# Expert weights and rows brought in at the ends of earlier stages, and a hidden transpose moved from TensorE to VectorE

## The reference, cut to what matters

```python
def ec_ffn(h, router_w, w_gate, w_up, w_down):
    cap = EC_CAPACITY_FACTOR * n_tok // N_EXPERTS
    aff = jax.nn.softmax((h @ router_w).astype(jnp.float32), axis=-1)
    top_aff, idx = lax.top_k(jnp.swapaxes(aff, 1, 2), cap)
    xg = jax.vmap(lambda hb, ib: hb[ib])(h, idx)
    hid = jax.nn.silu(xg @ w_gate) * (xg @ w_up)            # per expert, 1024 -> 512
    y = (hid @ w_down) * top_aff[..., None]                 # 512 -> 1024
    return zeros.at[idx].add(y)
```

```python
def hier_moe(h, w_rg, b_rg, w_re, b_re, w_up, w_down):
    grp = argmax(h @ w_rg + b_rg); p_grp = softmax(...)[grp]
    top_v, top_i = lax.top_k((h @ w_re + b_re)[grp], TOP_K)        # TOP_K = 2
    gate = jax.nn.softmax(top_v, axis=-1) * p_grp
    g, u = jnp.split(xb @ w_up[e], 2, axis=-1)                     # 1024 -> 2 x 512
    y = (jax.nn.silu(g) * u) @ w_down[e]                           # 512 -> 1024
    return segment_sum(y * gate, token)
```

## Time and profile before

| what | us |
|---|---|
| median of three runs (4654.29 to 4656.44) | 4656.21 |
| the profiled execution | 4653.48 |
| its span in the trace | 4651.7 |
| PE busy in the span | 4087.7 (88%) |
| DVE busy | 2057.1 (44%) |
| ACT busy | 1237.6 (27%) |
| POOL busy | 732.8 (16%) |
| data moved by DMA | 761.18 MB, mean 164 GB/s |

### The profile page before, as it was taken

The page is one execution under the profiler, slowest core; times in us unless marked ns, Lnnn a source line. Parts: engine busy times, 40 slices in busy tenths (PEclk is TensorE's granted clock), DMA queues, the critical chain, the costliest instruction groups (busy, mean ns, idle before and its releaser), DMA issues. The chain is left out here.

```text
span 4651.7 us, 76558 instructions
## 1 busy us (share of the span) xinstructions
PE 4087.7 (88%) x30623; PEld 2783.0 (60%) x30623; DVE 2057.1 (44%) x4137; ACT 1237.6 (27%) x2473; POOL 732.8 (16%) x851
## 2 busy tenths in 40 slices
PE   6998999976999799899986997999887987799995
PEld 4674557444887567566544885767565645455553
DVE  1223557126555322456425453121396676444443
ACT  1112346140000111335330001111265433233333
POOL 0110000301111011000201110000362050122221
PEclk8998999987999899999988998999898998899997
DMA  7115110357787511412138996210352102899996
GB/s 256 35 47 130 24 34 16 131 207 290 269 278 276 164 54 45 110 24 49 40 148 329 335 331 231 88 56 31 104 137 90 42 32 85 311 378 361 367 374 237
DMA packets 247019, 761.18 MB, mean 164 GB/s; under 512 B 60836, under 2 KB 137196, under 8 KB 233256
## 3 DMA queue, kind: packets, MB, share of 16 engines
q1 hardware_dynamic: 219240, 653.77, 39.2%
q0 software_dynamic: 21808, 81.80, 7.0%
q10 hardware_dynamic: 5712, 22.02, 1.2%
HBM read 646.28 MB, written 111.25 MB: 163 GB/s over the span
## 5 line engine op out<-in xcount | busy, mean ns | idle before, releaser
L627 PE MATMUL p_ring<-p_hT,p_wc 128*128 128x256 f32 x1008 | 220.3, 381 | 4.9 <-DMA p_wc<-in_w_in 4.9
L3507 ACT ACTIVATE bexp_y<-bexp_acc,slot_gates 32x256 f32<-32x256 f32 x384 | 178.8, 466 | 144.3 <-PE bexp_acc L3550 135.5
L3565 PE MATMUL bexp_gu<-bexp_wu,bexp_xT 128*32 128x256 f32 x3072 | 182.1, 395 | 39.1 <-DMA bexp_wu<-in_w_expert_up 34.6
L627 PEld LDWEIGHTS p_ring<-p_hT,p_wc 128*128 128x128 f32 x1008 | 192.2, 191 | 31.6 <-issue 5.3
L3565 PE MATMUL bexp_gu<-X,bexp_xT 128*32 128x256 f32 x3072 | 177.8, 389 | 14.5 <-DMA X<-in_w_expert_up 11.7
L3594 DVE TENSOR_SCALAR bexp_ex<-bexp_ex 128x128 f32<-128x128 f32 x96 | 53.3, 555 | 287.4 <-ACT bexp_ex L3515 287.3
L635 PE MATMUL p_ring<-p_wt,p_hT 128*128 128x400 f32 (+2 forms) x480 | 170.8, 516 | 0.0
L3565 PEld LDWEIGHTS bexp_gu<-bexp_wu,bexp_xT 128*32 128x32 f32 x3072 | 101.4, 114 | 114.3 <-issue 58.5
L1119 PE MATMUL l0mla_scores<-l0mla_kT,l0mla_qT 96*128 96x512 f32 (+1 forms) x312 | 143.0, 547 | 21.0 <-DMA l0mla_qT<-RT 15.2
L2029 PE MATMUL l0exp_gu<-l0exp_xT,l0exp_wg 128*128 128x160 f32 x1024 | 154.4, 304 | 4.5 <-DVE l0exp_xT L2073 4.5
L3565 PEld LDWEIGHTS bexp_gu<-X,bexp_xT 128*32 128x32 f32 x3072 | 98.9, 112 | 87.8 <-DMA X<-in_w_expert_up 17.1
(11 more groups left out here) (683 smaller groups left out, 8436.6 us busy)
## 6 DMA issues: line engine op xcount, KB each, us to landing
X<-in_w_expert_up SPq DMA_DIRECT2D x16, 4096.0 KB, 18.5
bexp_wu<-in_w_expert_up SPq DMA_DIRECT2D x16, 4096.0 KB, 18.5
l0exp_wg<-in_exp_w_gate SPq DMA_DIRECT2D x16, 2048.0 KB, 8.4
l0exp_wu<-in_exp_w_up SPq DMA_DIRECT2D x16, 2048.0 KB, 13.1
l0exp_wd<-in_exp_w_down SPq DMA_DIRECT2D x16, 2048.0 KB, 12.9
l1exp_wg<-in_exp_w_gate SPq DMA_DIRECT2D x16, 2048.0 KB, 8.8
l1exp_wu<-in_exp_w_up SPq DMA_DIRECT2D x16, 2048.0 KB, 13.1
l1exp_wd<-in_exp_w_down SPq DMA_DIRECT2D x16, 2048.0 KB, 13.9
```

What stands on the lines that cost most here:

```text
L627: mm = nc.tensor.matmul(out[:, i * PC:(i + 1) * PC], wc[:, k, b * 128:(b + 1) * 128], hT[ch % 2][:, k, :], start=(k == 0), stop=(k == KD - 1))
L3507: nc.scalar.activation(y[j][32 * r:32 * r + 32, c * YN:(c + 1) * YN], acc[rows_c, r // 2, r % 2, :], ACT.Copy, scale=gates[rows_c, r, bass ...
L3565: mm = nc.tensor.matmul(gu[r][32 * c:32 * c + 32, 0:2 * HN].rearrange("p (h n) -> p h n", h=2), xT[j][:, k, 32 * r:32 * r + 32], both[:, : ...
```

## The change

**First experts.** A class `FirstExpert` owns three 4 MB buffers `held` and a buffer of rows across both the route and the experts stage. The modulation weights of the route pass through `held`, each half of which is later one expert weight buffer; the rows' buffer is also the route's `hT0`. At the end of the route SP issues the weights of expert 0 once the modulation products that used those buffers are done, and POOL issues expert 0's gathers once the rows are stored and the choice is written. In the experts stage SP waits until they have landed and goes on with expert 1, and POOL gathers for expert 1.

```diff
+    def load(self, sp, multiplied, groups):
+        sp.wait_ge(multiplied, START + groups - 2)
+        sp.dma_start(self.wg[0], ...).then_inc(self.gate_in, 16)
+        sp.dma_start(self.wu[0], ...).then_inc(self.up_in, 16)
+        sp.wait_ge(multiplied, START + groups - 1)
+        sp.dma_start(self.wd[0], ...).then_inc(self.down_in, 16)
...
-                for n in range(N):
+                for n in range(N - 1):
                     mod.store(sp, n)
+                expert.load(sp, mod.multiplied, N)
+                mod.store(sp, N - 1)
                 mod.wait_end(sp)
-                for j in range(3):
-                    sp.wait_ge(stored[j], START + 16 * len(range(j, NT, 3)))
...
                 for n in range(N):
                     mod.finish(po, n)
+                for j in range(NX):
+                    po.wait_ge(stored[j], START + 16 * len(range(j, NT, NX)))
+                po.wait_ge(final_taken, START + 2 * len(sets))
+                expert.gather(po, XN)
...
-                for e in range(E):
+                sp.wait_ge(gathered[0], 16 * NS)
+                for e in range(1, E):
...
-                for e in range(B):
-                    gather(e)
+                gather(1)
```

```diff
+                act.dma_start(first_up[0], w_up[0]...).then_inc(first_in[0][0], 16)
+                for e in range(2):
+                    act.dma_start(first_down[e], w_down[e]...).then_inc(first_in[1][e], 16)
                 act.wait_ge(eps_made, START + 1)
...
-                step(V_.tensor_scalar(nb[:, :], cnt[:, 0:N_EXP], 0.0, None, ALU.is_gt))
-                for q in range(1, -(-SEQ // BLOCK)):
-                    step(V_.scalar_tensor_tensor(nb[:, :], cnt[:, 0:N_EXP], float(BLOCK * q), nb[:, :], ALU.is_gt, ALU.add))
+                step(V_.tensor_tensor(counted_over[:, :, :], over..., cnt..., ALU.is_lt))
+                step(V_.tensor_reduce(more[:, :], counted_over[:, :, :], AX.X, ALU.add))
...
+                    po.wait_ge(steps, START + marks[f"blocks{half}"])
+                    nc.gpsimd.tensor_tensor(pair[:, part, 1, :], in_block[:, part, :], gate..., ALU.mult).then_inc(spread, 1)
...
-                sp.wait_ge(steps, START + marks["first"])
+                sp.wait_ge(squares, START + T)
                 sp.wait_ge(spilled, START + 16 * T)
-                sp.dma_start(first_w[0], w_up[e]...); sp.dma_start(first_w[1], w_down[e]...)
+                sp.dma_start(first_up[1], w_up[1]...).then_inc(first_in[0][1], 16)
```

```diff
-                with sp.Fori(1, pairs) as i:
-                    for j in range(B):
-                        ...
+                load_up(1, 0)
+                with sp.Fori(1, last) as i:
+                    load_up(i, 1)
+                    load_down(i, 0)
+                    load_up(i + 1, 0)
+                    load_down(i, 1)
+                load_up(last, 1)
+                load_down(last, 0)
+                load_down(last, 1)
...
-                        if r == 0 and not first:
-                            hid_turn(i + j - 1, 1 - j)
...
+                        nc.vector.tensor_tensor(hidR[j][:, r, :].rearrange("p (f n) -> p f n", f=4), ex[r][:, :].rearrange("p (n f) -> p f n", f=4),
+                                                gu[r][:, HN:2 * HN].rearrange("p (n f) -> p f n", f=4), ALU.mult).then_inc(steps[j], 1)
+                        wait_alone(ve, steps[j], base + 4, passed_ve)
                         if r == 0:
-                            wait_alone(ve, hid_turned[j], LOOPED + i, passed_ve)
-                        nc.vector.tensor_tensor(hidR[j][:, r, :], ex[r][:, :], gu[r][:, HN:2 * HN], ALU.mult).then_inc(steps[j], 1)
+                            wait_alone(ve, downed[j], LOOPED + i * R, passed_ve)
+                        nc.vector.transpose(hid[j][:, r, :], hidR[j][:, r, :]).then_inc(steps[j], 1)
```

292 lines of the change are left out of this document (160 added, 132 removed).

## The result

The changed kernel takes 4614.07 us in the median of four runs (4612.94 to 4618.06), a ratio of 0.9911 to the kernel before, which took 4656.32 beside it (95% interval 0.9897 to 0.9925): 42 us less, where 56 were forecast. The time lies inside the range of 4578 to 4627, but outside the forecast's own of 4588 to 4608, and inside the prices of the rival in which the stream of weights gets no faster (4611 to 4616). The profiled execution has a span of 4611.4 us against 4651.7, so 40.3 us less.

The account below looks back on a forecast made before the run. The weight stream, not PE, was taken to set the block experts' period. From 4653.48 us, -18.7 + 1.9 - 38.9 - 0.6 = -56.3 gave 4597.2, forecast as 4600; own range 4588 to 4608, wider range 4578 to 4627.

Parts of the forecast that it names:

- The seams: Between route and expert stages, earlier gathers on quiet DMA engines gain 10.1 us at the first and 8.6 at the second.
- Dispatch: Dispatch stage: ACT's issues +1.1, load collision +2, DVE work -0.8, tail -0.4; net +1.9 us, bounds -2 and +6.
- The lock between POOL's product and DVE: In dispatch, POOL's gate product and DVE's two-SBUF-input steps exclude each other, giving back 1.2 us a half.
- The start of the stream: Block experts' start: block 3's up weights land at +44.7 us after up(0), instead of +58.2; lead 13.5 us.
- The period: Block experts: time a block falls from 19.22 to 18.3 us, 25.8 us over 28 blocks; bounds 17.6 and 18.9.
- the skipped rows: Block experts: empty slots no longer gathered, 1024 of 3072 rows, save 0.52 us a block.
- the order of SP's loads: Block experts: loads issued as buffers come free remove 0.5 us of empty DMA time a block.
- Rival (a): Block experts: bytes set the period, the stream gets no faster; period 18.7 to 18.9, 4611 to 4616 us; chance 0.22.
- (b): Block experts: stream period falls to 17.6 or less and PE's 17.1 sets it; 4574 to 4582 us; chance 0.12.
- (c): Dispatch and seams: 8.4 MB of weights delay router loads, XN's stores or gate store; +6 to +12 us; chance 0.12.
- (d): Block experts: DVE's transposes delay PE, slower than before from 1.6 us each; 4694 us at 2.0; chance 0.04.
- (e): More than 32 blocks, +37 us a pair, or gathers still wait for weights, +10 to +18; chance 0.05.

Follow-up runs that it names:

- e7: The changed kernel with the route and expert stages of the kernel before: 4635.05 us.
- e4: The changed kernel with SP issuing the block experts' loads in the order of the kernel before, up and down of a block together: 4648.68 us.
- e10: The changed kernel with down buffers padded by 32 bytes between rows, so one DMA per down load goes in 4 KB pieces: 4597.94 us.
- e3: The changed kernel with each down load in two DMAs of 1 MB, in 4 KB pieces: 4596.15 us.
- e2: The changed kernel with empty slots gathered too from block 2 on, from rows 0 to 95: 4623.34 us.
- e8: The changed kernel with every transpose on DVE done a second time, into a tile nothing reads: 4612.73 us.
- e6: The changed kernel with down weights in 4 KB pieces, and up weights too, in two DMAs of 2 MB each: 4609.67 us.
- e5: The changed kernel with each down load in two DMAs, in 8 KB pieces: 4603.66 us.
- e9: The changed kernel with each down load in two DMAs of 64 partitions, in 16 KB pieces: 4887.7 us.
- e11: The changed kernel, empty slots left out of the scatter, blocks 0 and 1's weights loaded by SP after the last XN store, expert table after slot_rows: 4606.24 us.
- e1: The changed kernel with empty slots left out of the block experts' scattering DMA too: 4615.83 us.

## Why the prediction was right in its range, and where it was wrong

*The seams: right.* Forecast 10.1 and 8.6, measured 10.4 and 8.3 in the profile, 10.3 and 8.4 by e7. The 4.9 us of a gather on quiet engines, read from another stage, carried it. It was a little long: from the start of the issue to PE's first transpose it is 3.65 us for the context gather (1095.31 to 1098.96) and 4.44 at the second seam. At the first seam this made up for a term that was put at nothing: POOL's first issue begins 0.93 us after DVE's last copy ends (1092.89 to 1093.82).

*Dispatch: right within its bounds, with one size off.* ACT's issues and the traffic at the start cost 3.0 us up to the first step of DVE on the counts (84.33 us after the stage's start, 81.35 before), where 3.1 were put down; that it is so near is luck, since the same code has 88.0 in e4, 6.6 over the kernel before. From there to the first transposes of the block experts the stage is 2.6 us shorter (23.34 against 25.94), where 1.2 were. The lock between POOL's product and DVE costs 0.58 us a half, not 1.2: of DVE's two steps beside it the first, which began at 3949.43, 0.04 us ahead of POOL's, took its usual 0.61, and only the second one was longer (1.54 in place of 0.96). The Trainium skill, *SBUF — State Buffer*, section "Who interferes with whom", has a VectorE instruction with two SBUF inputs contend with a GpSimd instruction that reads SBUF, and the order of issue decide which of the two is held up; the trace agrees (the step ahead of POOL's took 0.61 us, the one behind it 1.54).

*The start of the stream: right, but its lead was lost on the way.* Block 3's load goes out 31.5 us after the first up product (4000.45 - 3968.99), forecast 29 to 31, and lands 14.0 us later, at +45.5, forecast +44.7 (the load's row in the DMA table: count, KB, median us to landing):

```profile
X<-in_w_expert_up SPq DMA_DIRECT2D x1, 4096.0 KB, 14.0
```

up(3) begins at +54.9 (4023.90) and waits for DVE's xT by 0.62 us and not for weights. But up(31) begins at +572.8 (4541.83), not at +557: from block 3's landing on, a block takes (572.8 - 45.5) / 28 = 18.83 us, where 18.3 were put down. So nearly all of the block experts' miss, 15.8 us up to up(31), lies in the period; the end of the stage gives 1.5 back. The 18.56 between SP's issues is the smaller number because a load's way from issue to use grows meanwhile, to 24.6 us for block 31 (4517.23 to 4541.83).

*The period: wrong in three sub-steps, not all of one sign.* The sentence that failed is "I take 18.3, as contiguous 16 KB pieces of the down weights can only help". They cost 0.6 to 0.7 us a block: with the same kernel and pieces of 4 KB, the size that the kernel before has, the stage is 585.5 (e10) or 588.5 (e3) in place of 604.3, 16 to 19 us, which is the 14 us by which the forecast missed and a little more. With them the forecast's 590.0 us for the stage would have been met. The 403 GB/s of the earlier trace rows were measured on 4 KB pieces of down weights at a DMA share of 0.97 and taken over for 16 KB pieces in a full stream, where q1 has 392; the trace of before could not show what that would cost, and e4 shows that such a rate doesn't hang on the pieces alone. The second sub-step that failed is the skipped rows. Half a microsecond a block was put down for them, and the period shows none of it for the gathers (18.53 in e2, 18.55 and 18.56 with the rows left out). What made up for this is the order of SP's loads, which was worth 0.9 us a block (19.46 in e4 against 18.56) where 0.5 of empty time were put down. That the time still fell into the range is in part the luck of this third miss. The three do not add up to the change from 19.22 to 18.56: -0.9 for the order and 0.6 to 0.7 for the pieces leave 0.4 to 0.5 of its 0.66 without a run, and the price of the pieces was measured in the new order only. Nor is the sum of the two queues' shares, 18.71 us a block or 18.2 with the skipped rows, the floor that the forecast took it for: in e3 and e10 a block takes 17.8 to 18.0 us, and in e10 the two shares add up to 101.8% of the time.

*Rival (a)* gave the right time, 4611 to 4616, and half the right reason. The skipped rows save no time that shows, as it says, and the weights of a block, 6.29 MB, move in 18.7 us (148.29 MB in 440), its 18.7 to 18.9. But there is no ceiling of 368 GB/s: the changed kernel moves 372, e10 388 on the same mix. The Trainium skill, *DMA: Bandwidth & Descriptors*, section "Specifications", has 368 as the vendor's derate and some 358 for a core's HBM limit; these runs lie above both.

*The other rivals.* PE as the bound (b): not reached, PE waits for weights in every version, 28.6 us in e10. Contention in dispatch (c): there, but at the forecast's own price in the changed kernel (3.0 us of 3.1), and 3.5 over it in e4. Slower by DVE's turns (d): e8 rules it out. That it doesn't do what it says (e): the gathers land early, and 32 blocks run.

What stays open: why pieces of 16 KB make the stage longer, while the up weights are faster in 32 KB than in 4 (e6). e5, e3 and e10 order the sizes for the down weights alone; no run tells a cause, nor whether the weights' own rate or the gathers that land late beside them is the first link.

## What to carry to other kernels

A rate that is read from a trace belongs to the shape of the transfers it was read from; when a change also alters the pieces of a transfer, the rate is a new unknown with bounds on both sides, even where larger pieces seem sure to be better. In a stage whose transfers set the time, first fill the queue in the order in which buffers come free (32 us here), then try the size of the pieces (16 to 19 us), and expect little from bytes saved on another queue. Busy shares of queues that overlap don't add up to a floor. And run the same stage twice before reading 2 or 3 us of it as an effect.

## What the runs showed of the hardware that was not expected

- The size of the pieces of the down weights, in a mix with 4 MB up loads, gathers and scatters: 392 GB/s on the weights' queue at 16 KB, 403 at 8 KB, 405 to 406 at 4 KB; with the up weights cut from 32 to 4 KB as well, 394. All of these at a DMA share of 1.01 to 1.03; at a share of 0.93 (e4) 16 KB pieces went at 409.
- Two transfers of 64 partitions in place of one of 128 took the mixed stream from 372 to 239 GB/s at a DMA share of 1.01 (e9).
- With 8.4 MB on ACT's queue in flight, SP's issue of a small broadcast load lasted 18.51 us (1.04 before, 1.51 in e11, where these loads come later); every other small load and F's first three stores stood behind it. In e11 DVE's first step on the counts begins 80.75 us after the stage's start, against 84.33 in the changed kernel and 88.0 in e4; ACT's first copy begins 1.9 us earlier there than in the changed kernel.
- Behind a wait of 1.78 us for a gather, TensorE's granted clock was 0.50 and a down product took 6.94 us in place of 5.39. In e10, whose waits for weights last 1.8 us at most, the stretch of 440 us has a granted clock of 1.00.
- Rows left out of an indirect DMA shorten its queue's share (14.8% to 11.5% in e1), but hardly the time of what runs beside it.
